# One gather per layer for a grouped-expert layer, and weights in long runs, on one Trainium2 core

## The reference

```python
def trunk_layer(x, cond, p, router_w, router_bias, ...):
    mod = (jnp.matmul(jax.nn.silu(cond), p['w_ada']) + p['b_ada'])[:, None, :]
    sh1, sc1, g1, sh2, sc2, g2 = jnp.split(mod, 6, axis=-1)
    h = rmsnorm(x, p['norm1']) * (1 + sc1) + sh1
    q, k, v, gq, gk, gv, gg, lr_f, lr_b, ga, gb = _split_proj(jnp.matmul(h, p['w_in']))
    ...
    merged = jax.nn.sigmoid(ga) * jnp.matmul(o_attn, p['w_pa']) + jax.nn.sigmoid(gb) * jnp.matmul(o_gla, p['w_pb'])
    x = x + g1 * jnp.matmul(merged, p['w_out'])
    h2 = rmsnorm(x, p['norm2']) * (1 + sc2) + sh2
    x = x + g2 * grouped_moe(h2, router_w, router_bias, p['w_gate'], p['w_up'], p['w_down'])

def grouped_moe(h, router_w, router_bias, w_gate, w_up, w_down):
    ...
    gates = jnp.sum(jax.nn.one_hot(top_idx, N_EXPERTS) * top_w[..., None], axis=1)
    act = jax.nn.silu(jnp.einsum('nd,edf->nef', hf, w_gate)) * jnp.einsum('nd,edf->nef', hf, w_up)
    return jnp.einsum('nef,efd->nd', act * gates[..., None], w_down)
```

## Time and profile before

| | |
|---|---|
| median of 3 runs | 1128.09 us (1126.59 to 1129.05) |
| the profiled execution | 1133.62 us, of it 1131.6 us span |
| TensorE busy | 1043.7 us, 92% of the span |
| VectorE, ScalarE, GpSimd busy | 354.9, 221.1, 87.1 us |
| DMA | 312.15 MB in 136431 packets, 73.7% of the engines' span on SP's queue |
| expert pairs, layer 0 | 346 to 585 us |
| expert pairs, layer 1 | 890 to 1128 us |

### The profile page before, as it was taken

One profiled execution on the slowest core, in us unless ns is written; L12 is line 12 of the kernel. 1 busy time (PEld: TensorE's weight loads), 2 busy tenths in 40 slices (PEclk: granted clock), 3 DMA queues, 4 the chain that ended last, 5 costly groups with the idle time before them and its releaser, 6 DMA issues.

```text
span 1131.6 us, 13595 instructions
## 1 busy us (share of the span) xinstructions
PE 1043.7 (92%) x5214; PEld 618.9 (55%) x5214; DVE 354.9 (31%) x930; ACT 221.1 (20%) x461; POOL 87.1 (8%) x52
## 2 busy tenths in 40 slices
PE   5899999978969999999999999998797899999997
PEld 2348876646835444444444687766585544444442
DVE  2124123762151222222240411167425222222222
ACT  1103223311131111111131222241103111111110
POOL 0000005620000000000000000255100000000000
PEclk9999999989988999999999999998898899999999
DMA  9985334079787999989999632242369399999994
GB/s 360 395 302 188 102 123 149 1 283 343 278 327 290 395 395 379 386 331 396 392 391 325 222 130 94 75 149 100 132 242 377 141 395 395 392 376 355 361 392 175
DMA packets 136431, 312.15 MB, mean 276 GB/s; under 512 B 4096, under 2 KB 6272, under 8 KB 136128
## 3 DMA queue, kind: packets, MB, share of 16 engines
q1 hardware_dynamic: 135808, 309.14, 73.7%
q0 software_dynamic: 576, 2.36, 0.5%
HBM read 309.65 MB, written 1.84 MB: 275 GB/s over the span
## 4 chain that ended last, share of the span: by engine, by line
PE 83%; DVE 9%; ACT 2%; DMA 2%; issue 2%; SPq 1%; DVEq 0%; ACTq 0%
PE ps L801 20%; PE ps L815 10%; PE ps L449 10%; PE ps L533 7%; PE ps L769 6%; PE ps L707 5%; PE ps L853 4%; PE ps L638 3%; PE ps L696 3%; PE ps L551 2%; PE ps L623 2%; PE ps L462 2%; DMA ring<-w_in 2%; PE ps L429 2%; DVE x L1495 1%
## 5 line engine op out<-in xcount | busy, mean ns | idle before, releaser
L801 PE MATMUL ps<-ring,tmq 128*64 128x512 f32 x928 | 209.4, 594 | 0.0
L881 ACT ACTIVATE tmq<-ps 128x512 f32<-128x512 f32 (+3 forms) x152 | 74.2, 490 | 320.2 <-PE ps L533 89.5
L801 PEld LDWEIGHTS ps<-ring,tmq 128*64 128x64 f32 x928 | 67.5, 137 | 124.2 <-issue 124.1
L1495 DVE SCALAR_TENSOR_TENSOR x<-ps,mod,x 128x128 f32<-128x128 f32 x256 | 69.1, 344 | 180.5 <-PE ps L853 180.5
L815 PE MATMUL ps<-ring,tmq 128*64 128x512 f32 x512 | 116.9, 598 | 2.0 <-ACT tmq L881 2.0
L449 PE MATMUL ps<-more,ring 128*128 128x256 f32 x512 | 114.3, 381 | 0.5 <-ACT more L881 0.5
L449 PEld LDWEIGHTS ps<-more,ring 128*128 128x128 f32 x512 | 96.1, 190 | 16.8 <-issue 3.8
L533 PE MATMUL ps<-ring,more 128*128 128x512 f32 (+1 forms) x256 | 99.1, 548 | 3.1 <-DMA ring<-w_in 3.1
L533 PEld LDWEIGHTS ps<-ring,more 128*128 128x128 f32 x256 | 48.8, 192 | 52.2 <-issue 47.0
L769 PE MATMUL ps<-tmq,sgb 128*128 128x128 f32 x512 | 67.6, 290 | 6.7 <-DVE tmq L1470 6.7
L853 PE MATMUL ps<-tmq 128*128 128x256 f32 x256 | 65.1, 393 | 5.7 <-DVE x L1495 5.7
(11 more groups left out here) (192 smaller groups left out, 954.3 us busy)
## 6 DMA issues: line engine op xcount, KB each, us to landing
ring<-w_down SPq DMA_DIRECT2D x64, 1024.0 KB, 14.1
ring<-w_gate SPq DMA_DIRECT2D x58, 1024.0 KB, 11.4
ring<-w_up SPq DMA_DIRECT2D x58, 1024.0 KB, 13.6
ring<-w_ada SPq DMA_DIRECT2D x24, 2048.0 KB, 9.1
ring<-w_in SPq DMA_DIRECT2D x16, 2048.0 KB, 17.6
ring<-w_out SPq DMA_DIRECT2D x4, 2048.0 KB, 8.5
ring<-w_pa SPq DMA_DIRECT2D x2, 2048.0 KB, 7.7
ring<-w_pb SPq DMA_DIRECT2D x2, 2048.0 KB, 8.6
```

The source lines that it names most:

```text
L801: mm = pe.matmul(ps[r:r + SLOTS, half, :].rearrange("p (j n) -> p j n", j=2), hg[:, k, r:r + SLOTS], gu_unit(l, kh, e, in_more)[:, :, kk, ...
L881: return act.activation(out, in_, ACT.Copy, scale=scale)
L1495: ins = dve.scalar_tensor_tensor(x[:, k, c], ps[:, 4 + f % 2, j * NT + s * T:j * NT + (s + 1) * T], mod[:, l, 40 + k, s:s + 1], x[:, k, c] ...
```

## The change

- **Gather.** It is done once a layer, ahead of the pairs. Each token has two rows, and all 512 rows are sorted by expert. VectorE makes one-hots for four chunks of 128 rows (`row_onehots`); TensorE gathers them (64 matmuls of 128 columns) into PSUM banks 2 to 5, ScalarE copies them into `hrows`, which lies over the late constants in `cst`. To place a row, TensorE also sums how many rows stand before each expert (`before_e`).
- **Windows.** For each pair ScalarE reads two starts from `starts` into registers and copies 64 rows for each expert from `hrows` to `hg` (`windows`). `posm` counts from the window's start.
- **Late constants.** As `hrows` overwrites them, SP loads them again in layer 1, ahead of the first unit of `w_in` gates.
- **Scatter.** The scatter of pair q - 1 stands in pair q, between the transposes of the two halves, and that of the last pair behind the loop. It goes over three PSUM banks (4, 5, 7, 4). The transposes of the gates stand at the end of their own pair. On VectorE the additions of pair q - 1 stand behind the activations of pair q.
- **Weights.** The host lays out every unit so that a partition's part of a DMA is contiguous: 16 KB for the dense units, 8 KB for each of the two DMAs of an expert unit. The bytes, units, slots and their order stay.

```diff
@@ SP @@
             def expert_unit(l, pr, u, full, in_more=False):
+                dst = expert_space(l, u, in_more)
                 for j in range(2):
+                    c = slice(j * UNIT // 2, (j + 1) * UNIT // 2)
                     if u < 4:
                         kh, e = u // 2, u % 2
-                        src = (w_gate, w_up)[j][l, bass.ds(pr * 2 + e, 1)].rearrange("o (k p) n -> p (o k) n", p=P)
-                        src, dst = src[:, kh * KH:(kh + 1) * KH, :], gu_unit(l, kh, e, in_more)[:, j]
+                        src = w_gu[l, bass.ds(pr * 2 + e, 1), kh, :, c]
...
+                    sp.dma_start(dst[:, c], src.rearrange("o p n -> p (o n)")).then_inc(full, 16)
...
+                    if l and ORDER[n] == (l, "gates", 0):
+                        sp.wait_ge(m_hg[l - 1], passes * (2 * PAIRS) + 1)
+                        sp.dma_start(cst[:, C_LATE:CW], consts[:, C_LATE:CW]).then_inc(in_d, 16)
@@ TensorE @@
+                pe.wait_ge(ada_mod, ada_before_experts(l) + len(win))
+                for c in range(ROWS // P):
+                    pe.wait_ge(row_onehot, (ROWS // P) * l + c + 1)
+                    for b in range(2):
...
+                                mm = pe.matmul(ps[:, 2 + 2 * (c % 2) + b, j * P:(j + 1) * P], h2tok[:, s, k * P:(k + 1) * P],
+                                               gg[:, s, c * P:(c + 1) * P], start=s == 0, stop=s == 1)
+                pe.wait_ge(row_copied, 2 * (ROWS // P) * (l + 1))
...
-                    for half in range(2):
+                    def turn(half):
...
-                        if not last:
-
-                            gather(pss, pr + 1, half)
+                    turn(0)
+                    if not first:
+                        scatter(q - 1)
+                    turn(1)
...
-                    if not last:
-                        turn_gates(q + 1)
-                        pe.wait_ge(m_hg[l], q * 2 + 5)
...
+                    turn_gates(q)
@@ ScalarE @@
+                def windows(q, pr):
+                    at = [act.value_load(starts[0:1, bass.ds(pr * 2 + e, 1)], min_val=0, max_val=LAST_WINDOW)
+                          for e in range(2)]
+                    act.wait_ge(m_gu[l][1], q + 1)
+                    for e in range(2):
+                        copy(hg[:, :, e * SLOTS:(e + 1) * SLOTS], hrows[:, :, bass.ds(at[e], SLOTS)]).then_inc(m_hg[l], 1)
@@ VectorE @@
+                def row_onehots(c):
+                    for s in range(S):
+                        g = gg[:, s, c * P:(c + 1) * P]
+                        ins = dve.tensor_scalar(g, C("slot"), chunk_rows[:, c, 0, s:s + 1], None, ALU.is_equal)
...
+                    activate(first)
+                    onehots(1, first + 1)
+                    with dve.Fori(1, PAIRS - 1) as pr:
                         q = pss * PAIRS + pr
+                        activate(q)
+                        add_experts(q - 1)
                         onehots(pr + 1, q + 1)
```

More of the change, by code:

```diff
@@ L73 @@
 D_W = LV_COLS + 2 * T
[L75 removed]
+CONSTS = [("ident", P), ("ones", P), ("before", P), ("slot", P), ("chunk", ROWS // P), ("cos", HD), ("sin", HD), ("order_g", NG),
           ("order_e", NE), ("dec_f", D_W), ("dec_b", D_W), ("mask", LV_COLS + T), ("side", LV_COLS)]
@@ L284, in unit_src @@
         def unit_src(key):
[L285 to L289, removed]
+            l, kind, n = key
             if kind in ("in", "gates"):
                 at, w = (IN_UNITS if kind == "in" else GATE_UNITS)[n]
[L292 to L295, removed]
+                return w_in[l, :, KT * at:KT * (at + w)]
+            if kind in ("ada", "out"):
+                return (w_ada if kind == "ada" else w_out)[l, n]
+            return (w_pa if kind == "pa" else w_pb)[l]
         def unit(key):
@@ L778, in turn_gates, with scatter, expert_pair @@
                     mm.then_inc(m_gwt[l], 1)
-                def expert_pair(pss, pr, in_more=False, later=False, last=False):
+                def scatter(q):
+                    pe.wait_ge(m_gwt_copied[l], q + 2)
+                    for f in range(4):
+                        if f % 2 == 0:
+                            pe.wait_ge(m_y[l], q * 2 + 2 + f // 2)
+                        if f in (0, 3):
+                            pe.wait_ge(m_x[l], q * 4 + (1 if f else 0) + X_DONE)
+                        for j in range(2):
+                            k = 2 * f + j
+                            mm = pe.matmul(ps[:, (4, 5, 7, 4)[f], j * NT:(j + 1) * NT], yy[:, k * P:(k + 1) * P], gwt,
+                                           start=True, stop=True)
+                        mm.then_inc(m_scat[l], 1)
+                def expert_pair(pss, pr, in_more=False, later=False, first=False):
                     q = pss * PAIRS + pr
@@ L1110, in expert_pair @@
                              ).then_inc(m_at_copied[l], 1)
-                        if not last:
-                            gathered(q + 1, half)
+                        if half == 0 and not last:
+                            windows(q + 1, pr + 1)
                     for n in range(2):
@@ L1115, in expert_pair @@
                         copy(yy[:, n * 512:(n + 1) * 512], ps[:, 2 + n, :]).then_inc(m_y[l], 1)
-                    if not last:
-                        turned_gates(q + 1)
+                    turned_gates(q)
                 with act.Fori(0, passes) as pss:
-                    for b in range(2):
-                        gathered(pss * PAIRS, b)
-                    turned_gates(pss * PAIRS)
+                    act.wait_ge(m_starts[l], pss + 1)
+                    act.sem_inc(m_begun[l], 1)
+                    windows(pss * PAIRS, 0)
                     with act.Fori(0, PAIRS - 1) as pr:
-                        expert_pair(pss * PAIRS + pr, False)
-                    expert_pair(pss * PAIRS + (PAIRS - 1), True)
+                        expert_pair(pss * PAIRS + pr, pr, False)
+                    expert_pair(pss * PAIRS + (PAIRS - 1), PAIRS - 1, True)
         @block.vector
```

217 lines of the change are left out of this document (132 added, 85 removed).

## The result

| | before | after |
|---|---|---|
| median | 1128.4 us (1126.59 to 1131.49, 8 runs) | 1137.8 us (1131.37 to 1139.26, 8 runs) |
| ratio | | 1.0063, 95% interval 1.0046 to 1.0081 |
| profiled execution, its span | 1133.62, 1131.6 us | 1136.47, 1134.6 us |
| first expert matmul, layer 0 and 1 | 346.25, 889.60 | 357.64, 902.92 |
| from there to the end of the last down matmul | 232.9, 232.9 | 223.1, 221.5 |

The change makes the kernel slower: by 9.4 us between the medians, and by 5.2 to 9.1 us by the interval of the ratio, where a gain of 3.8 was forecast. Where most of those 5.2 us are is shown with the experiments (run e11).

What follows compares the result with a forecast made beforehand. TensorE bounds the expert pairs (30.0 us each), the full DMA close behind (31.9). Layer 0 +17.8 - 16.8 = +1.0, layer 1 +13.9 - 16.8 = -2.9, start -1.9: sum -3.8, 1124.3 us, range 1109 to 1142.

Steps and rivals of the forecast that it cites:

- The start of the kernel: First w_in wait and modulation before the experts: faster weight transfers save 1.9 us.
- The start of the pairs in layer 0: First expert matmul 17.8 us later (364.0): one-hots +2.2, gather +10.6, gap before the first pair +5.0.
- The start in layer 1: First expert matmul 13.9 us later (903.5): earlier gather start -2.1, gather +11.1, gap +5.0.
- The transfers: Expert weights: longer rows raise the DMA rate from 394 to 422 GB/s, 4.97 us a unit.
- C: Rival: DMA rate rises little, stages stay at 410 GB/s, +5 us a layer, 1134; packet rule about 1138; chance 0.14.
- D: Rival: DMA rate doesn't rise at all, +11.2 us a layer and no gain at the start, 1149; chance 0.08.
- E: Rival: rate near 435 GB/s or start cheaper by 3 us, 1114; down to TensorE alone, 1103; chance 0.18.
- The pairs as a stage: From first expert matmul (t0) to the end of the last down matmul 215.0 us; gain 16.8 us a layer.
- the low clock in pair 0: First half pair: TensorE at 1.2 GHz behind 5 us of idleness, +2.0 us; first slot release at t0 + 8.9.
- the stall around pair 4: SP's queue stalls once, 1.8 us, where pair 4's down weights wait for a slot TensorE still holds.
- B: Rival: start costs more and TensorE falls to 1.2 GHz in DMA waits, +4 us a layer, 1132; chance 0.20.
- A: Likeliest case: all terms as summed, 1124.3 us, 1116 to 1130 with the errors of the start terms; chance 0.40.

Runs made afterwards that it cites:

- e11: Kernel before with the scatter one pair later and the gather kept in each pair, between the down halves, weights in old rows: 1128.9 us.
- e3: Changed kernel with SP issuing units 0 to 2 of pair 5 ahead of late units of pair 4: 1129.2 us.
- e7: Changed kernel with new unit order around pair 4, idle matmuls ahead of pair 0 and the table load ahead of the row copies: 1123.3 us.
- e9: Kernel before with long weight rows and the scatter one pair later, gather kept in each pair, measured a second time: 1115.9 us.
- e10: Kernel before with long rows, later scatter, gather kept in each pair, and units of pair 5 issued ahead of late ones of pair 4: 1115.7 us.
- e5: Changed kernel plus five idle matmuls on TensorE behind the row gather, ahead of pair 0: 1130.5 us.
- e12: Changed kernel with new unit order, idle matmuls ahead of pair 0, earlier table load, and idle matmuls inside pairs 1-3 and 5-7: 1131.0 us.
- e2: Changed kernel with the old layout of all weights (rows of 2 and 4 KB): 1162.5 us.

## Why the prediction went wrong

**The start of the kernel** (forecast -1.9): right. Late in the dense stages of layer 0 the matmuls of L706 (L696 before) start at 263.36 instead of 265.41.

**The start of the pairs in layer 0** (+17.8): near. The traces show +13.4 when the 2.0 above are taken off, but against e11, which has no low clock in the router, it is 357.64 - (343.14 - 2.05) = +16.6. The gather took 15.6 us (17.4 forecast), as the granted clock was at 1.00 from 340 on, 2.4 us into it where the forecast had 5.5; the gap behind it 4.5 (5.1).

**The start in layer 1** (+13.9): too much by 2.8. From the first dense matmul of the layer to the first expert matmul it is 308.65 (594.27 to 902.92) instead of 297.54 (592.06 to 889.60), +11.1. Gather 16.2 and gap 4.3 were 17.3 and 5.1 in the sum, and the gather started 0.9 earlier in the stage than forecast.

**The transfers** (422 GB/s, 4.97 us a unit): right, 421 and 422. Of the packets 36480 - 5072 = 31408 are of 8 KB and more (about 31,000 forecast). That strikes rivals C and D and the faster rate of E. By an estimate from the packet rule of the Trainium skill (DMA: Bandwidth & Descriptors, Why small descriptors are slow) the experts' mix would have gone to 405 only; the trace doesn't agree, and what a longer row saved is well above that overhead.

**The pairs as a stage** (t0 + 215.0): this is the step that failed. It measured t0 + 223.1 and t0 + 221.5. The gain of a layer was 9.8 and 11.4 us instead of 17.9, and three terms of the sum were too small or missing, here in layer 0:
- the low clock in pair 0 was priced at 2.0 us and took 3.0 (16.95 instead of 13.95); the first release came at t0 + 10.3 instead of t0 + 8.9: +1.4. In layer 1 it took 1.7, and the release came at t0 + 9.0;
- the stall around pair 4 was priced at 1.8 us, as one hole; it is two. The windows 458 to 464 and 466 to 470 move 238, 111, 389, 135 and 152 GB/s, which against 422 is 0.9 + 1.5 + 0.2 + 1.4 + 1.3 = 5.1 us: +3.3 (e3 gained 3.6 to 4.0 us there by removing most of it);
- behind the wait of 2.64 us in pair 7 the clock is low: 8.79 instead of 7.09 us, +1.7. The sum had nothing for it. It is rival B's mechanism, at close to B's price of 2.

These are 6.4 of the 8.1 us. In layer 1 the same three are +0.1, +3.3 and +1.4 (8.52), 4.8 of the 6.5. The rest isn't assigned: pair 7's second half starts in e7 at t0 + 195.5, where the walk through the units without stall and low clock gives 6.9 + 2.2 + 183.9 = 193.0, so about 2 us are left even there. Smaller holes (a slice of 416) may be part of them.

**The sum.** Forecast 1124.3. With the measured pairs, +8.1 and +6.5, and the measured starts, -1.2 and -2.8, it is 1134.9, beside 1136.5 of the profiled execution and 1137.8 of the median. 1.6 to 2.9 us stay unassigned. The longer tail behind the last down matmul (10.1 us to the end of the span, 9.1 before) isn't among them, since the forecast had 1.15 for it. The starts cost 4.0 us less than forecast, and the pairs missed 14.6 of their gain; the second is what turned the sign.

**The rivals.** B, at 1132, had the right sign and the right mechanism for the clock in pairs 2, 3 and 7, not for the start, which was cheaper than forecast. It was still short, since both A and B took the stall at 1.8 us, and that is nearly half of what the pairs lack (3.3 of 8.1). I had put the likeliest case together with a short stall and with no low clock behind a wait; each is small, and both act on the same chain and point one way. C's times, 1134 and 1138, lie nearest the measured one, by luck: its rate of 405 to 410 GB/s isn't in the trace.

**What the change's parts are worth**, from the runs: long rows and later scatter together gain 12.5 us (e9 against before), and the single gather gives 22 away (after against e9), though it has half the matmuls. Between the two traces it is 18.5: the starts cost 17.2 and 11.3 us, and the pairs give back only 4.3 and 5.9. In the pair the gather takes 3.8 us of 29.2 on TensorE, and a pair's weights take 6 x 4.97 = 29.8 us anyway; taken out, it is replaced by waits (L833's 29.2 us above). Ahead of the pairs it stands where the DMA is idle and nothing else goes on. Even with the repairs that gained (e7, 1123.3) the single gather stays 7.4 us behind e9.

## What to carry to other kernels

When two resources are within a few per cent, shorten the work of one only as far as the other allows. Work taken out of a stage that is bound by transfers is worth only what the transfers leave, and moved ahead of the stage it is paid in full if the transfers stand still there. Make a queue's walk unit by unit with the release of each slot, for every pair and not only for the last; a queue in program order stops at the first slot that isn't free, and the hole it makes comes back later if the stage waits for transfers (e3), and not if it doesn't (e10). Idle matmuls paid here where a wait was certain (e5) and cost their full time where there was none (e12). And before a gain of 1 us is put down to an edit, compare the clock of both traces ahead of the place that it changes (e3, e4).

## What the runs showed of the chip beyond that

- A wait of 2.6 us is not always followed by the lower clock. In e7 two halves behind such waits ran at the upper clock and one at the lower, in one trace:

```profile
418.59 7.09 PE L844 MATMUL ps<-ring,tmq 128*64 128x512 f32 x32 [2.66 <-DMA ring<-w_gu]
448.41 7.09 PE L844 MATMUL ps<-ring,tmq 128*64 128x512 f32 x32 [2.62 <-DMA ring<-w_gu]
553.38 8.71 PE L844 MATMUL ps<-ring,tmq 128*64 128x512 f32 x32 [2.68 <-DMA ring<-w_gu]
```

  In e2 a wait of 3.56 us was followed by 7.09, in e11 one of 2.01 by 8.78. What decides it stays open. The Trainium skill (TensorE: Matmul & The Clock Gate, HAM oscillation) tells of DMA waits of 3 to 5 us with the clock back at the lower level behind every one. Here it was so in part of them: of e2's five waits of 3.5 to 3.7 us three were followed by 7.09, and shorter ones could bring the lower clock.
- A transfer of 1 MiB in rows of 2 KB takes SP's queue 0.4 us behind a pause and up to 5.0 us in the pairs of layer 0 of before, while the DMA engines are full; in rows of 8 KB the median of after is 0.33. The timeline of e11:

```profile
407.14 2.98 SPq L347 DMA_DIRECT2D ring<-w_up  x1
410.32 4.60 SPq L347 DMA_DIRECT2D ring<-w_gate  x1
```

  Such issues are the SPq 11% in the chain of e2. No run shows that they cost time of their own, since the DMA was full meanwhile.
- Loading the late constants again in layer 1 (2112 KB) cost nothing that the traces show, as forecast: "between" is 322.2 us, 11.7 more than before, and the start of layer 1 (+11.1) with the last scatter of layer 0 (+0.6) account for it.
